# Heads started earlier by swapped buffers, a re-ordered prologue, chunk-wise waits and a final scaling on one engine, in a two-layer encoder trunk

## The chip, the cores and the metric

The kernel runs on one core of one Trainium2 chip. The core has TensorE (PE, matrix products, with its weight loads PEld), VectorE (DVE), ScalarE (ACT), GpSimd (POOL) and SyncE (SP), which here only issues DMAs. The metric is the device time of one execution in microseconds; the figure of a kernel is the median of several runs.

## The reference

Two request groups (prompt and sample), each one sequence of 512 tokens with 1024 features, go through the same two layers and a last RMSNorm. Both groups share all weights.

```python
def trunk(x, c, g_norm, w_ada, b_ada, g_final, even_p, odd_p):
    for l in range(DEPTH):
        mod = jax.nn.silu(c) @ w_ada[l] + b_ada[l]
        shift, scale, gate = jnp.split(mod, 3, axis=-1)
        h = rmsnorm(x, g_norm[l]) * (1 + scale[:, None, :]) + shift[:, None, :]
        j = l // 2
        if l % 2 == 0:
            out = even_mixer(h, *[p[j] for p in even_p])
        else:
            out = odd_mixer(h, *[p[j] for p in odd_p])
        x = x + gate[:, None, :] * out
    return rmsnorm(x, g_final)
...
def odd_mixer(h, w_in1, conv_w, conv_b, w_q, w_k, w_v, w_gate, b_gate, g_mh, skip, w_out1):
    xm, z = jnp.split(h @ w_in1, 2, axis=-1)
    xc = jax.nn.silu(centred_conv(xm, conv_w, conv_b))
    q = headwise(xc, w_q)
    k = headwise(xc, w_k)
    v = headwise(xm, w_v)
    pre = (jnp.concatenate([q, k, v], axis=-1) @ w_gate + b_gate).astype(jnp.float32)
    ...
    h_fwd = mlstm_scan(qh, kh, vh, i_f, jax.nn.log_sigmoid(f_f))
    h_bwd = flip(mlstm_scan(flip(qh), flip(kh), flip(vh), flip(i_b), flip(jax.nn.log_sigmoid(f_b))))
    hs = h_fwd + h_bwd
    ...
    out = (hn.astype(xm.dtype) + skip * xc) * jax.nn.silu(z)
    return out @ w_out1
```

`even_mixer` is one input projection, latent attention with 8 heads, neighbourhood attention with 8 heads, a SiLU gate and an output projection. `odd_mixer` is an mLSTM with 4 heads of 512 features, forward and backward in time, whose head outputs are normalised (`hn`).

## The kernel before

**Tiling.** Every activation is kept with features on the 128 partitions and the 512 tokens of a group in the free dimension (T = 512); x is 8 such chunks (DC = 8), the inner width of the mLSTM 16 (IC = 16). A product of two fp32 operands is made of three products: each operand is split into a high part (ACT, a copy with rounding) and a low part (DVE, a subtraction), and `three` (L483 to L485) multiplies high by high, low by high and high by low. So "hi_..." functions run on ACT, "lo_..." functions on DVE, and PE needs both.

**Weights** come as 81 blocks a group of 128x1024 through a ring of 3 slots (`stream_weights`, L478, SP). `act_split` (L457) writes w_hi and `dve_split` (L465) w_lo, one block each, two in advance (PAIRS = 2). PE multiplies a block with 24 products.

**Order.** There is no scheduler: each engine has a list written out by hand, and semaphores (`wait_ge`, `then_inc`) are all that joins the lists. An instruction that waits holds back everything behind it on its engine. The lists run group 0 (layer 0 in the a_ functions, layer 1 in the e_ functions), then group 1.

**Prologue** (`p_sync`, `p_tensor`, `p_scalar`, `p_vector`). PE transposes vectors (L369, L370), then makes the first modulation in 8 steps k (`ada_step`, L295: 8 product instructions of 2 columns by 512), each when a part of w_ada of 1 MB has come. Between them stand 16 "folds" (`fold`, L361 to L365), which multiply the headwise q, k, v weights into the gate weights; DVE feeds them by `expand` (L410) and stores them by `keep` (L415 to L417). `FOLDS[k]` says how many folds are done after step k. The first mean square is summed over chunks by POOL (`n_gpsimd`, L557, L560) from ACT's squares (`n_square`, L550), and PE adds over partitions by a product with ones (`n_tensor`, L565 and L567) at k = 5. `ada_turn` (L303) and `ada_evict` (L311) end the modulation, `dve_h` and `act_h` (L510, L521, L515) make the first h, and the first projection (L483) starts.

**mLSTM part** (functions inside the e_ part). For each head h PE does: keys (L1461) and token values (L1478) one head in advance, `scores` (kk by xc), `turn` (L1511, transposes of the weighted scores Pn), `values` (pt by v), `back` (L1529). ACT makes `decay` (L1613, L1617; exponentials into the tile Dm, from rows that POOL's `masked` L1389 writes), hi_keys (L1595), hi_values (L1600), pts (L1671), hi_u (L1630). DVE makes `weights(h, i)` (L1776 to L1792; scores times decay, the norm, and the normalised Pn), `stats` (L1798, L1801), lo_keys (L1759), lo_values (L1765), pts low (L1844), scaled_u (L1815), lo_u (L1807). POOL makes `split_x` (L1378, L1380), `skipped` (L1414), `times_z` (L1408) and `norm_factors` (L1396 to L1400). The z half of the input projection runs ahead of the heads and beside head 0: after z block c + 2's products ACT stores SiLU(c) (L1645) and splits the next block. `F_...` constants put gate work between them. Dm lies in the memory of ring slots 1 and 2; so the first decays wait for the last block of the ring (w_lo of block B_OUT1).

**Tail and end.** The last projection (B_OUT1 on, L483 with u_h) needs split blocks and u. `fin_tensor` (L579, L581), `fin_scalar` (L585, L587, L589), `fin_scale` (L597) and `fin_out` (L606) are the last RMSNorm: chunks 0 to 4 are scaled on DVE, 5 to 7 on POOL. For group 0 this runs inside group 1's first blocks.

## Time and profile before

| | |
|---|---|
| time, median of 3 runs | 1626.69 us (1623.75 to 1637.08) |
| time of the profiled execution | 1624.33 us |
| its span, first to last instruction | 1622.5 us |
| mean granted TensorE clock | 0.991 |
| PE busy | 1542.9 us (95%) |
| DVE, ACT, POOL busy | 873.3, 688.7, 375.8 us |
| chain that ended last, by engine | PE 82%, DVE 9%, ACT 5% |
| first projection product starts | 57.91 us |
| last projection product starts | 1606.34 us |

The page gives sums over the whole span. Where time is lost is seen in the waits of PE, a list that says for each line of PE what it waited for, how long in all, how often and how long at most, and in timelines of short stretches. A mean duration in a row with "x8" is the time of all 8.

### The profile page before, as it was taken

To read this page: it belongs to the slowest core of one execution; us is meant where nothing else is said; L and a number is where in the kernel's file an instruction comes from. 1 tells how busy PE (TensorE), PEld (TensorE's weight loads), DVE (VectorE), ACT (ScalarE), POOL (GpSimd) and SP (SyncE) were. 2 spreads that over 40 slices of the span, in tenths; PEclk is the share of its full clock that TensorE was granted. 3 is DMA by queue.
4 is the path that set the end of the run, shared out by engine and by line. 5 is a ranking of instruction groups with operands and counts; after the bars stand their busy time and mean duration, and the time that the engine had idled before them with its cause. 6 is when DMAs were issued, how large, how long until landed. Compare 5 with 4: busy or idle time off the path is not lost.

```text
span 1622.5 us, 19287 instructions
## 1 busy us (share of the span) xinstructions
PE 1542.9 (95%) x7334; PEld 1149.4 (71%) x7334; DVE 873.3 (54%) x1525; ACT 688.7 (42%) x1152; POOL 375.8 (23%) x434
## 2 busy tenths in 40 slices
PE   6999999999999998999999999999999999899996
PEld 4677755668777776777787885566877778677785
DVE  4523236664787427775543324576488751777433
ACT  1323235663533425443544333665443342544333
POOL 2011113332010013564311001342210002265312
PEclk9999999999999999999999999999999999999998
DMA  9288841112322331215334443021342233111421
GB/s 362 90 249 237 280 162 43 43 60 91 130 91 79 120 126 40 49 30 195 93 103 149 130 152 108 30 62 40 100 146 79 92 118 109 45 41 47 148 92 65
DMA packets 68987, 179.51 MB, mean 111 GB/s; under 512 B 20624, under 2 KB 21008, under 8 KB 66848
## 3 DMA queue, kind: packets, MB, share of 16 engines
q1 hardware_dynamic: 68896, 178.29, 34.1%
q8 instruction: 58, 0.95, 0.3%
q14 instruction: 33, 0.27, 0.1%
HBM read 153.59 MB, written 24.67 MB: 110 GB/s over the span
## 4 chain that ended last, share of the span: by engine, by line
PE 82%; DVE 9%; ACT 5%; issue 2%; DMA 1%; SPq 0%; DVEq 0%; ACTq 0%
PE ps L483 20%; PE ps L485 20%; PE ps L484 20%; PE ps L980 3%; PE ps L1029 3%; PE ps L1012 3%; PE ps L997 2%; PE ps L295 2%; DVE w_lo L465 1%; PE ps L911 1%; PE ps L1478 1%; PE ps L1461 1%; ACT w_hi L457 1%; PE ps L1300 1%; DMA at<-w_ada 1%
## 5 line engine op out<-in xcount | busy, mean ns | idle before, releaser
L465 DVE TENSOR_TENSOR w_lo<-at,w_hi 128x1024 fp32r<-128x1024 f32 x162 | 202.6, 1251 | 388.9 <-ACT w_hi L457 388.9
L457 ACT ACTIVATE w_hi<-at 128x1024 fp32r<-128x1024 f32 x162 | 170.4, 1053 | 120.3 <-PE ps L485 120.3
L483 PE MATMUL ps<-h_e_hi,w_hi 128*128 128x512 f32 x480 | 190.9, 398 | 7.9 <-DVE w_lo L465 7.9
L485 PE MATMUL ps<-h_e_hi,w_lo 128*128 128x512 f32 x480 | 187.0, 390 | 0.0
L484 PE MATMUL ps<-h_e_lo,w_hi 128*128 128x512 f32 x480 | 186.9, 389 | 0.0
L483 PE MATMUL ps<-h_a_hi,w_hi 128*128 128x512 f32 x400 | 160.4, 401 | 1.7 <-DVE h_a_lo L515 1.1
L484 PE MATMUL ps<-h_a_lo,w_hi 128*128 128x512 f32 x400 | 157.0, 393 | 0.0
L485 PE MATMUL ps<-h_a_hi,w_lo 128*128 128x512 f32 x400 | 156.8, 392 | 0.0
L1135 POOL TENSOR_SCALAR at<-at,at 128x512 f32<-128x512 f32 x128 | 87.0, 692 | 153.5 <-DVE at L1072 153.5
L483 PEld LDWEIGHTS ps<-h_e_hi,w_hi 128*128 128x128 f32 x480 | 90.1, 188 | 43.8 <-DVE at L1288 11.7
L485 PEld LDWEIGHTS ps<-h_e_hi,w_lo 128*128 128x128 f32 x480 | 90.1, 188 | 19.2
L483 PE MATMUL ps<-u_h_hi,w_hi 128*128 128x512 f32 x256 | 100.4, 392 | 3.4 <-issue 3.4
L484 PEld LDWEIGHTS ps<-h_e_lo,w_hi 128*128 128x128 f32 x480 | 90.2, 188 | 18.2 <-issue 0.5
L485 PE MATMUL ps<-u_h_hi,w_lo 128*128 128x512 f32 x256 | 99.7, 389 | 0.0
L484 PE MATMUL ps<-u_h_lo,w_hi 128*128 128x512 f32 x256 | 99.6, 389 | 0.0
L1288 DVE SCALAR_TENSOR_TENSOR at<-ps,at,at 128x510 f32<-128x510 f32 (+1 forms) x128 | 96.0, 750 | 4.5
L483 PEld LDWEIGHTS ps<-h_a_hi,w_hi 128*128 128x128 f32 x400 | 75.8, 190 | 28.9 <-issue 9.4
L1389 POOL TENSOR_TENSOR at<-at,at 128x512 f32<-128x512 f32 x16 | 22.0, 1395 | 290.8 <-DMA at<-a_rows 290.8
L485 PEld LDWEIGHTS ps<-h_a_hi,w_lo 128*128 128x128 f32 x400 | 75.8, 189 | 16.3
L484 PEld LDWEIGHTS ps<-h_a_lo,w_hi 128*128 128x128 f32 x400 | 75.8, 190 | 15.7 <-issue 0.7
L1012 PEld LDWEIGHTS ps<-at,at 128*128 128x128 f32 x512 | 56.7, 141 | 36.2 <-issue 32.0
L1012 PE MATMUL ps<-at,at 128*128 128x128 f32 x512 | 71.8, 278 | 7.4 <-ACT at L1112 7.2
(257 smaller groups left out, 3024.3 us busy)
## 6 DMA issues: line engine op xcount, KB each, us to landing
at<-blocks_in SPq DMA_DIRECT2D x162, 512.0 KB, 3.7
at<-w_ada SPq DMA_DIRECT2D x32, 512.0 KB, 4.9
at<-w_ada SPq DMA_DIRECT2D x8, 1024.0 KB, 18.5
z_kept<-at SPq DMA_DIRECT2D x32, 256.0 KB, 2.2
at<-z_kept SPq DMA_DIRECT2D x32, 256.0 KB, 2.8
at<-t_masked SPq DMA_DIRECT2D x16, 448.0 KB, 3.3
at<-xs SPq DMA_DIRECT2D x2, 2048.0 KB, 9.6
sg_kept<-at SPq DMA_DIRECT2D x16, 256.0 KB, 4.5
```

What stands on the lines that cost most here:

```text
L295: last = pe.matmul(ps(ADA_BANK[p])[32 * q:32 * q + G], siluc[:, G * k:G * k + G], parts[q], start=(k == 0), stop=(k == DC - 1))
L457: act.activation(whi[:, n % PAIRS], wring[:, n % SLOTS], ACT.Copy).then_inc(sem("w_hi"), 1)
L465: dve.tensor_tensor(wlo[:, n % PAIRS], wring[:, n % SLOTS], whi[:, n % PAIRS].bitcast(F32), ALU.subtract)\
L483: pe.matmul(o, stationary[0], moving[0], start=first, stop=False)
L484: pe.matmul(o, stationary[0], moving[1], start=False, stop=False)
L485: return pe.matmul(o, stationary[1], moving[0], start=False, stop=final)
L980: last = pe.matmul(ps(s_bank(j) + e), qcat[0:QK, u, m * P:(m + 1) * P], kcat[0:QK, u], start=True, stop=True)
L997: last = pe.matmul(ps(s_bank(j + e) + m), naq[a][r:r + 64, n, col:col + P], nak[b][r:r + 64, n], start=(s == 0), stop=(s == 2))
L1012: last = pe.transpose(ps(4 + q)[:, col:col + P], Pt[:, j % 4, e, s * P:(s + 1) * P], ident)
L1029: last = pe.matmul(ps(6 + n % 2)[64 * e:64 * e + 64, 2 * P * half:2 * P * half + 2 * P], v[:, s, (2 * n + e) % HEADS], PT[(j - 1 + e) % 4] ...
L1135: last = pool.tensor_scalar(Pt[:, j % 4, e], Pt[:, j % 4, e], rinv[:, n:n + 1], 1.0, ALU.mult, ALU.mult)
L1288: dve.scalar_tensor_tensor(y[:, lo:hi], src[:, lo + d:hi + d], vb("convw", t * IC + c), y[:, lo:hi], ALU.mult, ALU.add).then_inc(sem("e_co ...
```

## The change

It has six parts.

1. Prologue: `FOLDS` puts more folds ahead and none behind the last modulation; `expand` runs six ahead of `keep`, and the first two `dve_split` stand ahead of keep(14). The mean square is made of eight products with ones on PE, two at each of k = 1 to 4, without POOL. `busy` adds three 128x512 products on a tile of zeros, one ahead of the vector transposes and two behind.
2. The memory of Dm and Pn is swapped. Decays (0,0) and (0,1) move from behind z block 14 to behind z block 13, without the wait for w_lo; decays (1,0) and (1,1) move behind pts(0). On ACT hi_keys(1) goes ahead of decay (0,3), and the split of block B_Z + 17 behind it; its DVE half goes behind weights (0,3). The loads of the last projection wait for the last turn.
3. Token values of head 0 are made in the order 0, 1, 3, 2; `scores` and `values` wait for each chunk of kk and pt instead of for all four.
4. On DVE lo_keys(h+2) and lo_values(h+1) stand ahead of weights(h+1, 3) for h = 0 and 1.
5. Tail: on ACT the split of the second block stands behind the first two hi_u, and the squares of the next x behind the splits.
6. The final scaling is all on DVE, the outputs go out in the order 0 to 7; the 128x1 activations that loaded a table become table loads.

```diff
-    Pn = chunks(take(4 * T, at=L1 + 16 * T), T)
+    Dm = chunks(take(4 * T, at=L1 + 16 * T), T)
...
-    Dm = chunks(take(4 * T, at=ring_lo + 2 * T), T)
+    Pn = chunks(take(4 * T, at=ring_lo + 2 * T), T)
...
-    FOLDS = (1, 4, 6, 8, 10, 12, 14, 14)
+    FOLDS = (4, 6, 8, 10, 12, 14, 16, 16)
...
+        def busy(n):
+
+            for _ in range(n):
+                pe.matmul(ps(4), Weff[:, 0:4], Weff[:, 0:16], start=True, stop=True)
+
+        pe.wait_ge(sem("p_zero"), 2)
+        busy(1)
         pe.wait_ge(sem("p_rows"), 32)
         pe.transpose(ps(0)[:, 0:P], rows[:, 0], ident)
         pe.transpose(ps(0)[:, P:2 * P], rows[:, 1], ident).then_inc(sem("p_vecT"), 1)
+        busy(2)
         pe.wait_ge(sem("p_silu"), 1)
         folded = 0
         for k in range(DC):
             pe.wait_ge(sem(f"p_w{k}"), 16)
             ada_step(pe, 0, k, [ada_w[k][:, q * T:(q + 1) * T] for q in range(4)])
-            if k == 5:
-                groups[0].n_tensor(pe, 6)
+            if 1 <= k <= DC // 2:
+                for c in range(2 * k - 2, 2 * k):
+                    pe.wait_ge(sem("nx_sq"), c + 1)
+                    pe.matmul(ps(6), cst("ones"), nsq[:, c % 2], start=(c == 0), stop=(c == DC - 1))\
+                        .then_inc(sem("nx_add" if c < DC - 1 else "nx_ms"), 1)
             for c in range(folded, FOLDS[k]):
                 fold(c)
             folded = FOLDS[k]
         ada_turn(pe, 0)
-        for c in range(folded, IC):
-            fold(c)
...
+        for c in range(6):
+            expand(c)
         for c in range(IC):
-            expand(c)
-        for c in range(12):
+            if c == IC - 2:
+                for b in range(PAIRS):
+                    groups[0].dve_split(dve, b)
             keep(c)
-        for b in range(PAIRS):
-            groups[0].dve_split(dve, b)
+            if c + 6 < IC:
+                expand(c + 6)
         ada_evict(dve, 0)
-        for c in range(12, 14):
-            keep(c)
         ada_add(dve, 0)
         dve.wait_ge(sem("mod_set"), 3)
         dve.wait_ge(sem("rstd_done"), 1)
         groups[0].dve_h(dve, 0, 0, h_A, xT)
-        for c in range(IC - 2, IC):
-            keep(c)
...
             sp.wait_ge(sem("g_s"), at("g_s", 4 * ML_H))
-            sp.wait_ge(sem("g_P"), at("g_P", 8 * ML_H))
-            sp.wait_ge(sem("g_Pn"), at("g_Pn", 4 * ML_H))
+            sp.wait_ge(sem("g_t"), at("g_t", 4 * ML_H))
             stream_weights(sp, B_OUT1)
...
             def scores(h, part):
-                pe.wait_ge(sem("g_kk"), at("g_kk", 4 * h + 4))
                 pe.wait_ge(sem("g_xs"), at("g_xs", 4 * h + 4))
                 for i in part:
                     if h > 0:
                         pe.wait_ge(sem("g_P"), at("g_P", 8 * (h - 1) + 2 * (i + 1)))
                     for c in range(HC):
+                        if i == 0:
+                            pe.wait_ge(sem("g_kk"), at("g_kk", 4 * h + c + 1))
...
             def values(h):
                 pe.wait_ge(sem("g_v"), at("g_v", 4 * h + 4))
-                pe.wait_ge(sem("g_pt"), at("g_pt", 4 * h + 4))
                 for m in range(TM):
                     for s in range(TM):
+                        if m == 0:
+                            pe.wait_ge(sem("g_pt"), at("g_pt", 4 * h + s + 1))
...
-                if c == IC - 2:
-                    act.wait_ge(sem("w_lo"), at("w_lo", B_OUT1 + 1))
+                if c == IC - 3:
                     decay(0, 0)
                     decay(0, 1)
+            hi_values(0)
             decay(0, 2)
-            hi_values(0)
+            hi_keys(1)
             decay(0, 3)
-            hi_keys(1)
+            act_split(act, B_Z + IC - 1 + PAIRS)
             for h in range(ML_H):
-                if h + 1 < ML_H:
+                if 0 < h < ML_H - 1:
                     decay(h + 1, 0)
                     decay(h + 1, 1)
                 for s in range(TM):
                     act.wait_ge(sem("g_t"), at("g_t", 4 * h + s + 1))
                     act.activation(pts[0][:, s], ps(4 + s), ACT.Copy).then_inc(sem("g_ph"), 1)
+                if h == 0:
+                    decay(1, 0)
+                    decay(1, 1)
...
             act_split(act, B_TAIL + PAIRS)
-            hi_u(ML_H - 1)
+            hi_u(ML_H - 1, (0, 1))
             for b in range(B_TAIL + 1, B_END):
...
                 act_split(act, b + PAIRS)
+                if n == 1:
+                    hi_u(ML_H - 1, (2, 3))
...
                 stats(h, 3)
+                if h + 2 < ML_H:
+                    lo_keys(h + 2)
+                    lo_values(h + 1)
                 if h + 1 < ML_H:
                     weights(h + 1, 3)
                 if h > 0:
                     lo_u(h - 1, (3,))
-                if h + 2 < ML_H:
-                    lo_keys(h + 2)
+                if h + 2 == ML_H:
+                    lo_values(h + 1)
                 if h + 1 < ML_H:
-                    lo_values(h + 1)
                     scaled_u(h)
...
-            for j in range(5):
+            for j in range(DC):
                 LAST.fin_scale(dve, j)
```

Three places of the engines' lists show what stands where. In all of them a line number of the changed kernel differs by a few from the one before; at_... names are memory tiles.

The first is PE's list in the prologue, from its start. Before, L369 and L370 are the vector transposes, L295 a modulation step, L361 to L365 a fold:

```order
L369 MATMUL ps<-at_1808_49,at_256_78 128x128
L370 MATMUL ps<-at_1808_49,at_256_78 128x128
L295 MATMUL ps<-at_2048_70,at_16_54 2x512 x4
L361 MATMUL ps<-at_6144_69 128x128
L362 MATMUL ps<-at_1808_49,at_6144_69 128x128
L363 MATMUL ps<-at_962_79,at_6144_69 128x16
L364 MATMUL ps<-at_962_79,at_6144_69 128x16
L365 MATMUL ps<-at_962_79,at_6144_69 128x16
L295 MATMUL ps<-at_2048_71,at_16_54 2x512 x4
```

The same place of the change (L366 is `busy`, L294 the modulation, L356 to L360 a fold):

```order
L366 MATMUL ps<-at_1024_60 128x512
L371 MATMUL ps<-at_1808_49,at_256_77 128x128
L372 MATMUL ps<-at_1808_49,at_256_77 128x128
L366 MATMUL ps<-at_1024_60 128x512 x2
L294 MATMUL ps<-at_2048_69,at_16_54 2x512 x4
L356 MATMUL ps<-at_6144_68 128x128
L357 MATMUL ps<-at_1808_49,at_6144_68 128x128
L358 MATMUL ps<-at_962_78,at_6144_68 128x16
L359 MATMUL ps<-at_962_78,at_6144_68 128x16
L360 MATMUL ps<-at_962_78,at_6144_68 128x16
```

Behind the fourth fold the second modulation step follows, and behind it the first pair of mean-square products (L382):

```order
L359 MATMUL ps<-at_962_78,at_6144_68 128x16
L360 MATMUL ps<-at_962_78,at_6144_68 128x16
L294 MATMUL ps<-at_2048_70,at_16_54 2x512 x4
L382 MATMUL ps<-at_1024_111,at_1808_49 128x512 x2
L356 MATMUL ps<-at_6144_68 128x128
L357 MATMUL ps<-at_1808_49,at_6144_68 128x128
```

So the mean square's products move from behind step 5 to behind steps 1 to 4, and products on zeros stand ahead of all.

The second is DVE's list at the boundary of heads 0 and 1, from the end of the statistics to scaled_u. Before:

```order
L1798 BN_STATS at_24_158<-ps 128x6
L1801 BN_AGGR at_8_159<-at_24_158 128x2
L1776 SCALAR_TENSOR_TENSOR at_2048_145,at_8_157<-ps,at_2048_145 128x512
L1776 SCALAR_TENSOR_TENSOR at_2048_145,at_8_157<-ps,at_2048_145 128x128
L1782 SCALAR_TENSOR_TENSOR at_8_161<-at_8_157,at_64_156 128x2
L1783 TENSOR_TENSOR at_8_157<-at_8_157,at_8_161 128x2
L1784 RECIPROCAL at_8_157<-at_8_157 128x2
L1788 TENSOR_SCALAR at_2048_140<-at_2048_145,at_8_157 128x512
L1792 SCALAR_TENSOR_TENSOR at_2048_140<-at_2048_145,at_8_157,at_2048_140 128x128
L1759 TENSOR_TENSOR kk_g_lo<-ps,kk_g_hi 128x512 x4
L1765 TENSOR_TENSOR v_g_lo<-ps,v_g_hi 128x512 x4
L1815 SCALAR_TENSOR_TENSOR at_8192_127<-ps,at_128_51,at_8192_127 128x512 x4
```

And now:

```order
L1801 BN_STATS at_24_157<-ps 128x6
L1804 BN_AGGR at_8_158<-at_24_157 128x2
L1762 TENSOR_TENSOR kk_g_lo<-ps,kk_g_hi 128x512 x4
L1768 TENSOR_TENSOR v_g_lo<-ps,v_g_hi 128x512 x4
L1779 SCALAR_TENSOR_TENSOR at_2048_139,at_8_156<-ps,at_2048_139 128x512
L1779 SCALAR_TENSOR_TENSOR at_2048_139,at_8_156<-ps,at_2048_139 128x128
L1785 SCALAR_TENSOR_TENSOR at_8_160<-at_8_156,at_64_155 128x2
L1786 TENSOR_TENSOR at_8_156<-at_8_156,at_8_160 128x2
L1787 RECIPROCAL at_8_156<-at_8_156 128x2
L1791 TENSOR_SCALAR at_2048_144<-at_2048_139,at_8_156 128x512
L1795 SCALAR_TENSOR_TENSOR at_2048_144<-at_2048_139,at_8_156,at_2048_144 128x128
L1818 SCALAR_TENSOR_TENSOR at_8192_126<-ps,at_128_51,at_8192_126 128x512 x4
```

The low halves of keys and values have moved ahead of weights (1,3).

The third is ACT's list around the last z blocks. Before (L1645 is the SiLU, L457 a split, L1613 and L1617 decays, L1600 high values, L1595 high keys):

```order
L1645 ACTIVATE at_1024_144<-ps 128x512
L457 ACTIVATE w_hi<-at_3072_67 128x1024
L1645 ACTIVATE at_1024_144<-ps 128x512
L457 ACTIVATE w_hi<-at_3072_67 128x1024
L1613 ACT_TABLE_LOAD
L1613 ACTIVATE at_2048_145<-at_512_146,at_64_156 128x128
L1613 ACTIVATE at_2048_145<-at_512_147,at_64_156 128x128
L1617 ACTIVATE at_2048_145<-at_1024_148,at_64_156 128x384
L1613 ACTIVATE at_2048_145<-at_512_146,at_64_156 128x128
L1617 ACTIVATE at_2048_145<-at_1024_148,at_64_156 128x128
L1613 ACTIVATE at_2048_145<-at_512_147,at_64_156 128x128
L1617 ACTIVATE at_2048_145<-at_1024_148,at_64_156 128x256
```

Now:

```order
L1642 ACT_TABLE_LOAD
L1642 ACTIVATE at_1024_143<-ps 128x512
L460 ACTIVATE w_hi<-at_3072_66 128x1024
L1642 ACTIVATE at_1024_143<-ps 128x512
L1597 ACTIVATE v_g_hi<-ps 128x512 x4
L1610 ACT_TABLE_LOAD
L1610 ACTIVATE at_2048_139<-at_512_145,at_64_155 128x128
L1614 ACTIVATE at_2048_139<-at_1024_147,at_64_155 128x256
L1610 ACTIVATE at_2048_139<-at_512_146,at_64_155 128x128
L1614 ACTIVATE at_2048_139<-at_1024_147,at_64_155 128x128
L1592 ACTIVATE kk_g_hi<-ps 128x512 x4
L1610 ACTIVATE at_2048_139<-at_512_145,at_64_155 128x128
```

The last SiLU has no decays and no table load ahead of it any more, the high values come directly behind it, the high keys ahead of decay (0,3), and the last split, which stood behind the last SiLU, is not among these rows.

## Rows read from the trace of the kernel before

**Rows 1.** the page's part 1, busy time of each engine

```profile
PE 1542.9 (95%) x7334; PEld 1149.4 (71%) x7334; DVE 873.3 (54%) x1525; ACT 688.7 (42%) x1152; POOL 375.8 (23%) x434
```

**Rows 2.** waits of PE: engine, tile, line <- waited for: us, times, longest

```profile
PE ps L1478 <- DVE kk_g_lo L1759: 9.7, 4, 2.7
...
PE ps L295 <- DMA at<-w_ada: 8.2, 2, 4.4
...
PE ps L1461 <- DVE v_g_lo L1765: 1.9, 1, 1.9
PE ps L483 <- DVE pt_g_lo L1844: 3.7, 2, 1.8
PE ps L483 <- issue: 1.3, 1, 1.3
PE ps L1478 <- ACT at L1645: 3.3, 2, 1.7
PE ps L1511 <- DVE at L1792: 3.2, 2, 1.9
```

**Rows 3.** timeline, PE, prologue: start, us, what [idle before <- releaser]

```profile
8.63 1.89 PE L295 MATMUL ps<-at,at 128*2 128x512 f32 x8 [3.85 <-DMA at<-w_ada]
...
16.95 1.89 PE L295 MATMUL ps<-at,at 128*2 128x512 f32 x8 [4.39 <-DMA at<-w_ada]
...
52.28 1.04 PE L295 MATMUL ps<-at,at 128*2 128x512 f32 x8
...
57.91 0.77 PE L483 MATMUL ps<-h_a_hi,w_hi 128*128 128x512 f32 x1 [1.05 <-DVE h_a_lo L515]
```

**Rows 4.** chain that ended last, prologue: start us, us, what

```profile
24.70 1.81 PE ps L295 x8
30.47 1.81 PE ps L295 x8
...
43.83 2.00 PE ps L565 x2
45.83 1.54 PE ps L567 x2
```

**Rows 5.** windows: stretch, us, busy of PE, PEld, DVE, ACT, POOL, PEclk, DMA

```profile
650.00:700.00 50.00, 45.05 (x211) 35.29 (x210) 35.93 (x86) 21.75 (x42) 33.28 (x44) 0.96 0.19 42
```

**Rows 6.** timeline, ACT, around z block 14's SiLU, group 0

```profile
611.50 0.60 ACT L1645 ACTIVATE at<-ps 128x512 f32<-128x512 f32 x1 [15.12 <-PE ps L485]
...
615.00 0.70 ACT L1613 ACTIVATE at<-at,at 128x128 f32<-128x128 f32 x2 [0.66 <-DVE w_lo L465]
```

**Rows 7.** timeline, PE: scores of head 1, turn of head 1

```profile
629.41 0.50 PE L483 MATMUL ps<-kk_g_hi,xc_g_hi 128*128 128x512 f32 x1 [1.41 <-DVE kk_g_lo L1759]
...
673.51 1.91 PE L1511 MATMUL ps<-at,at 128*128 128x128 f32 x16
```

**Rows 8.** timeline, DVE: weights (1,3), low keys; 128x2 operation elsewhere

```profile
655.02 0.69 DVE L1776 SCALAR_TENSOR_TENSOR at<-ps,at 128x512 f32<-128x512 f32 x1 [1.89 <-PE ps L485]
...
655.97 1.13 DVE L1782 SCALAR_TENSOR_TENSOR at<-at,at 128x2 f32<-128x2 f32 x1
...
659.80 2.47 DVE L1759 TENSOR_TENSOR kk_g_lo<-ps,kk_g_hi 128x512 fp32r<-128x512 f32 x4
...
730.38 0.41 DVE L1782 SCALAR_TENSOR_TENSOR at<-at,at 128x2 f32<-128x2 f32 x1
```

**Rows 9.** timeline, POOL: masks of head 0, xc_g_lo, masks of head 2

```profile
585.89 3.26 POOL L1389 TENSOR_TENSOR at<-at,at 128x512 f32<-128x512 f32 x2 [127.50 <-DMA at<-a_rows]
...
655.82 1.26 POOL L1380 TENSOR_TENSOR xc_g_lo<-at,xc_g_hi 128x512 fp32r<-128x512 f32 x1
...
662.95 2.50 POOL L1389 TENSOR_TENSOR at<-at,at 128x512 f32<-128x512 f32 x2
```

**Rows 10.** DVE: the final scaling's timeline row; durations of L1807 (min/median/max)

```profile
1613.01 6.30 DVE L597 TENSOR_TENSOR at<-at,at 128x512 f32<-128x512 f32 x5 [5.48 <-ACT at L589]
...
L1807 DVE TENSOR_TENSOR u_h_lo<-at,u_h_hi x32: 657/681/1772, 684.5 to 1536.2; 128x512 fp32r<-128x512 f32 x32
```

103 lines of the change are left out of this document (47 added, 56 removed).

## The prediction

> **What bounds the kernel now.** I read the busy times first, then what PE waits for, then single stretches. PE is busy for 1542.9 of 1622.5 us [rows 1], so at most some 80 us can come from waits, and more only where a product itself takes too long. Next, PE's waits [rows 2]: the largest stand in the mLSTM part of each group and in the prologue. They belong to single rows of a list: token values (L1478) wait 9.7 us in 4 places for the low halves of the keys on DVE, 3.3 us for ACT's SiLU; keys (L1461) 3.8 us for the low halves of the values; turn (L1511) 3.2 us for DVE's weights (L1792), values (L483) 3.7 us for pt_g_lo, the last projection 3.4 us ("issue"), the modulation (L295) 8.2 us for w_ada. The counts of 2 and 4 say once or twice per group. Third, the durations in the prologue [rows 3]: the same 8 modulation products take 1.89 us at 16.95 and 1.04 us at 52.28. In the chain [rows 4] they start every 5.77 us (24.70, 30.47): 1.81 for them and 3.96 for two folds, so 1.98 each. The work runs at about half the later pace, 1.2 instead of 2.4 GHz as I read it, until the mean square's two products (43.83 and 45.83, 3.54 us [rows 4]) have ended; from then on everything takes half.
>
> **The change, part by part, for PE's time.**
>
> *Prologue.* Before, PE does modulation k, then folds, and one pair of mean-square products at k = 5; the first projection starts at 57.91 [rows 3]. After, four pairs stand at k = 1 to 4, two folds of 1.98 stand no longer behind the last modulation but ahead of it, and three products on zeros are added at the start. The three zeros' products cost about 1.75 us each at low clock (half of 3.54 [rows 4]); they end before w_ada's first part is there, at 8.63 [rows 3], which hides them; without that cover they would cost 5.3. w_ada's second part lands at 16.95 as before, since loads and their order on SP are the same. From there I go step by step. A k with a pair costs 1.81 + 3.54 + 3.96 = 9.3 at low clock and about half, 4.7, at high; one with two folds alone 5.8 or 3.0; k = 7 has 1.0. After the last modulation come 4.6 us of turn, addition and the first h, as the trace has between 53.3 (52.28 and 1.04) and 57.9 [rows 3]. If the clock is high once the first pair is done: 16.95 + 1.8 + 3.5 + 2.0 = 24.3, three k of 4.7 = 38.4, then 3.0 + 3.0 + 1.0 = 45.4, + 4.6 = 50.0, that is −7.9. If only the second pair raises it: 26.2 after k = 1, 33.5 after k = 2, 42.9, 49.9, + 4.6 = 54.5, −3.4; and +1.4 in either case if k = 0's four folds run at low clock (8.63 + 1.9 + 7.9 = 18.4, past 16.95). If it is high from 16.95 on: 47.4, −10.5. If it never rises: 18.4 + 4 × 9.3 + 2 × 5.8 + 1.8 + 4.6 = 73.5, +15.6. In the trace one pair sufficed, but 20 us of unbroken work stood ahead of it, where the new first pair has a wait. So I take **−5**, the middle of −7.9 and −1.9. The six further products cost 10.5 us at low clock, and that is the part's danger; POOL's sums, which they replace, ran beside PE and give nothing back.
>
> *Start of the heads.* Before, ACT waits for w_lo at 615.00 and does 2.5 us of decays between z block 14 and the last SiLU, for which token values (0) wait 1.7 at the longer place, then keys (1) 1.9 for the values' low halves, and scores (1) start at 629.41 after 1.41 more [rows 2, 6, 7]. After, these decays run behind z block 13, in the 15.12 us in which ACT is idle, and POOL has their masked rows ready (585.89 and 3.26 [rows 9]). Token values and keys run unbroken, −3.6; hi_keys(1) now stands behind decay (0,2) with its table load (about 1.3 + 1.3), ends its first chunk near 625.3, and scores (1), which now wait chunk by chunk, start at 625.5: −3.9. Behind them turn's wait of 1.2 shrinks by 0.7: **−4.6**. Split 66 moves behind decay (0,3); its block is consumed only at the tail. With the swap, Pn lies where blocks stream in later, so on SP the loads for the last projection now wait for the last turn (g_t) instead of the last weights, some 2 us (one turn) later; queued behind them are the last z_back and the next x, and all of them are wanted only after values (3): 0, and 2 if the tail had no slack.
>
> *Boundaries of heads 0 to 1 and 1 to 2.* Before, DVE does weights (1,3) from 655.02 to 659.8, then lo_keys for which token values wait [rows 8]; that wait is 2.4 in the mean, 2.7 at most [rows 2]. After, the low keys follow ACT's chunks at once and PE goes on as soon as the keys' banks are free: the wait goes, and so does part of the low clock behind it (the mean granted clock of this stretch is 0.96 [rows 5], 4 us at half pace, 2 lost). Wait and half pace are 4.4 together; followed through the lists, scores (2) start 3.1 to 3.7 sooner, since the keys' last bank then sets the start. New: weights (h+1,3), 4.8 us, stand behind the low values, which end at about 663.9, so they end at 668.7, and turn, which started at 673.51 [rows 7], wants them at about 669.9. I take **−3.4** per boundary.
>
> *Values of head 3*: the g_pt wait for each chunk removes three of four pt_g_lo operations (3.7 in 2 places [rows 2]): **−1.85**. *Tail*: before, ACT does all of hi_u and two squares ahead of split 68, and PE waits 3.4 in 2 places, 2.1 in the longer [rows 2]; after, split 68 follows two hi_u: **−2.1** in group 0, **−1.3** in group 1.
>
> Group 0: 4.6 + 2 × 3.4 + 1.85 + 2.1 = 15.35. Group 1, which repeats it: 14.55. Together 29.9; I take 28, half a us off for each of four boundaries, because the margin of 1.2 us at turn is thin.
>
> *Final scaling.* DVE's five take 6.30 us beside POOL's three; a two-input product of that shape takes 0.681 alone [rows 10], so eight take 5.4: with the last output then **−1.2** (bounds 0 and −1.6). In group 1 they hide under projections, DVE having room there; uncovered, three more would cost 2.0. The table loads stand in the same places; the 128x1 activation saves 0.1 to 0.2.
>
> **Sum**: −5 −28 −1.2 −0.2 = −34.4 from the profiled 1624.33 us: 1589.9, so 1590. The median shown is 1626.69, the fastest 1623.75; the profiled execution is between, so no shift is made.
>
> **A rule against the change.** DVE's 128x2 operation took 1.13 us at 655.97 and 0.41 at 730.38 [rows 8], and POOL was at two-input work of 1.27 us beside the former [rows 9]. The Trainium skill, "SBUF — State Buffer", section "Who interferes with whom", says that a DVE instruction with two SBUF inputs and a GpSimd instruction that reads SBUF exclude one another for a whole instruction. That agrees with these two rows.
>
> **Rivals.**
>
> (a) *The prologue stays at low clock.* For: 20 us of folds and modulation never raised it, and PE still waits until 16.95. Against: one pair did. Then +15.6 instead of −5: **1610.5**.
>
> (b) *Weights (h+1,3) come late.* POOL's masks at 662.95 take 2.50 for two [rows 9] and more POOL work follows, now beside the moved weights. Uncontended, weights take some 3.3 (the 1.13 would be 0.41, and its 512-wide scaling, lengthened likewise, is about as long as the 0.69 of the first row); with a POOL instruction of 1.27 ahead of three of them, 7.1. Then they end at 671.0, 1.1 after turn wants them, and low clock again costs 1.7 behind such a wait: 4 × 2.8 = 11.2 less gain: **1601**.
>
> (c) *The order does not matter*, because each wait returns at the next dependence. The waits of 1 to 2 us in a row at 616 to 636 speak for that, the chunk-wise waits against. The prologue and end alone stay: **1618**.
>
> (d) *Slower*: DVE falls behind at each boundary, low values waiting for ACT behind decays with weights and scaled_u queued behind. It loses the 13.6 there and adds a stall per boundary; the sum is 1603.5 plus four stalls. Slower than before it gets from 5.2 us a boundary, by over 1% from 9.3. With 8 us and 4 of half pace behind each (2 lost): **1643**. The longest wait in [rows 2] is 4.4, and it is for a DMA.
>
> **Numbers.** Forecast 0.62, (a) 0.13, (b) 0.17, (c) 0.05, (d) 0.03. About 1% (16.2 us) can be told from no change: 1608 to 1641 counts as the same. Forecast and (b) are faster, (a) is split: its own 1610.5 is inside, but falls under 1608 where the heads give 31: 0.06 faster, 0.07 same; (c) same; (d) slower. Faster 0.85, same 0.12, slower 0.03. The low end: −10.5 in the prologue, −33 (all listed waits of the heads and their low clock), −1.8: **1579**. The high end is (a): **1610**.
>
> **What would show it.** Prologue: the first modulation at 8.6 or later, the time of L295 x8 at k = 2, 3 (1.0 or 1.8) and the first projection near 53. Heads: L1478's waits near 0 in both groups, scores (1) near 4 us sooner after the last z block, L1511's wait small (if 4 us or more, (b)). Tail: no "issue" wait over 0.5. End: from the last L589 to the last L597 5.4 us instead of 7. The forecast is wrong if L295 stays at 1.8 past k = 3, or if turn's wait grows by over 2 us in several places.

## The result, and the profile after

| | before | changed |
|---|---|---|
| time, median | 1626.76 us (4 runs, 1623.75 to 1637.08) | 1580.28 us (4 runs, 1578.71 to 1580.83) |
| span of the profiled execution | 1622.5 us | 1578.2 us |
| PE busy | 1542.9 us (95%) | 1529.7 us (97%) |
| mean granted clock | 0.991 | 0.994 |

The ratio is 0.9723, with a 95% interval from 0.9701 to 0.9745: 2.8% faster, 44.3 us by the two spans and 46.5 by the medians, where 34.4 was forecast. The kernel before was run again beside each set of experiments and came out at medians of 1622.3 to 1625.4 us; the experiments are therefore compared with the changed kernel's 1580.28, and where 1 or 2 us matter, by their traces.

The page's first part answers to [rows 1]:

```profile
PE 1529.7 (97%) x7352; PEld 1138.6 (72%) x7352; DVE 873.2 (55%) x1531; ACT 689.2 (44%) x1148; POOL 352.4 (22%) x421
```

PE has 13.2 us less busy time with 18 product instructions more. A change of order alone cannot do that; these are products that no longer run at half clock. PE's waits, the view of [rows 2] (us in total, times, longest):

```profile
PE ps L486 <- DVE w_lo L468: 8.5, 9, 1.3
PE ps L1006 <- ACT at L1106: 7.2, 18, 0.9
...
PE ps L486 <- DVE h_a_lo L518: 3.0, 1, 3.0
...
PE ps L1526 <- DVE v_g_lo L1768: 2.5, 2, 1.3
...
PE ps L486 <- DVE kk_g_lo L1762: 2.2, 2, 1.1
PE ps L1507 <- DVE at L1795: 1.2, 2, 0.6
PE ps L1526 <- ACT at L1619: 1.1, 2, 0.9
```

Two of the rows shown in [rows 2] are those of group 1 alone. Over the whole span of the kernel before, which is what the prediction's text uses, they are:

```profile
PE ps L1461 <- DVE v_g_lo L1765: 3.8, 2, 1.9
PE ps L483 <- issue: 3.4, 2, 2.1
```

The largest row of before, 9.7 us of token values for the low keys, is gone, and with it the waits for the last SiLU, for v_g_lo at the keys, for pt_g_lo and "issue". What heads the list now, 8.5 us for w_lo and 7.2 for L1106, was there before with 8.6 and 7.2 and is not touched by the change. Two rows have grown: h_a_lo, 3.0 for 1.1, since no fold fills that gap now, and back's wait for L1619, which is new.

The prologue on PE, the view of [rows 3]:

```profile
8.46 1.04 PE L294 MATMUL ps<-at,at 128*2 128x512 f32 x8 [1.10 <-DMA at<-w_ada]
...
15.73 1.33 PE L294 MATMUL ps<-at,at 128*2 128x512 f32 x8 [2.10 <-DMA at<-w_ada]
16.99 3.35 PE L382 MATMUL ps<-at,at 128*128 128x512 f32 x4
...
22.18 1.04 PE L294 MATMUL ps<-at,at 128*2 128x512 f32 x8
...
48.21 0.76 PE L486 MATMUL ps<-h_a_hi,w_hi 128*128 128x512 f32 x1 [2.98 <-DVE h_a_lo L518]
```

The first modulation step takes 1.04 us, not 1.89: PE is at the high clock when it starts. Behind the wait of 2.10 at 15.73 it falls once (a pair takes 3.35), and from 22.18 to the end of the modulation everything is at full pace. The first projection starts at 48.21, and behind its wait of 2.98 it begins at half pace, as before.

In the heads, first the window of [rows 5] (stretch, us, busy of PE, PEld, DVE, ACT, POOL, PEclk, DMA share, GB/s):

```profile
650.00:700.00 50.00, 49.79 (x254) 40.77 (x254) 43.82 (x109) 25.60 (x53) 34.63 (x42) 1.00 0.18 53
```

PE's timeline, the view of [rows 7]: scores of head 1, turn of head 0 and turn of head 1.

```profile
617.09 0.47 PE L486 MATMUL ps<-kk_g_hi,xc_g_hi 128*128 128x512 f32 x1 [1.08 <-DVE kk_g_lo L1762]
...
623.44 1.97 PE L1507 MATMUL ps<-at,at 128*128 128x128 f32 x16 [0.62 <-DVE at L1795]
...
656.17 1.91 PE L1507 MATMUL ps<-at,at 128*128 128x128 f32 x16
```

DVE's timeline at the boundary of heads 0 and 1, the view of [rows 8]:

```profile
646.75 0.69 DVE L1768 TENSOR_TENSOR v_g_lo<-ps,v_g_hi 128x512 fp32r<-128x512 f32 x1 [0.20 <-ACT v_g_hi L1597]
...
650.04 0.68 DVE L1779 SCALAR_TENSOR_TENSOR at<-ps,at 128x512 f32<-128x512 f32 x1
...
650.98 1.13 DVE L1785 SCALAR_TENSOR_TENSOR at<-at,at 128x2 f32<-128x2 f32 x1
...
653.75 0.66 DVE L1795 SCALAR_TENSOR_TENSOR at<-at,at,at 128x128 f32<-128x128 f32 x1
```

The granted clock is 1.00 where it was 0.96, and PE is busy for 49.79 of 50 us where it was 45.05. The low values (L1768) and, ahead of them, the low keys now come before weights (1,3), which run from 650.04 to 654.4; turn starts at 656.17, 1.8 us behind them. The 128x2 operation at 650.98 takes 1.13 us as before: it is late in a place where nobody waits.

The end, the view of [rows 10]:

```profile
1570.27 4.91 DVE L599 TENSOR_TENSOR at<-at,at 128x512 f32<-128x512 f32 x8 [5.39 <-ACT at L593]
```

Eight scalings in 4.91 us where five took 6.30.

Where the 44.3 us of the span went is read by milestones, the start of the same products in both traces:

| stretch | before, us | changed, us | difference | forecast |
|---|---|---|---|---|
| start to first projection | 57.91 | 48.21 | −9.7 | −5 |
| to token values (0), group 0 | 558.83 | 560.47 | +1.6 | 0 |
| token values (0) to turn (0) | 19.78 | 14.76 | −5.0 | −4.6 |
| turn (0) to turn (1) | 36.99 | 32.73 | −4.3 | −3.4 |
| turn (1) to turn (2) | 37.51 | 32.64 | −4.9 | −3.4 |
| turn (2) to turn (3) | 25.56 | 25.84 | +0.3 | 0 |
| turn (3) to back (3) | 20.80 | 20.06 | −0.7 | −1.85 |
| back (3) to token values (0), group 1 | 622.90 | 620.37 | −2.5 | −2.1 |
| the same five stretches of group 1's heads | 141.40 | 125.40 | −16.0 | −13.25 |
| back (3) to the end | 100.82 | 97.72 | −3.1 | −2.7 |

The five stretches of group 1 are −7.4, −2.6, −4.9, +0.3 and −1.4. The forecast column adds up to −36.3; the prediction took 1.9 off that for the boundaries.

The first two rows hold for these two executions and vary from one execution to the next. Seven of the experiments below keep the changed kernel's prologue as it is: in their traces the first projection starts at 48.60 to 49.68 and token values (0) at 608.15 to 610.76, where the changed kernel's trace has 48.21 and 608.68. Behind token values (0) the traces are steadier. From there to the end of the span the kernel before needs 1005.76 us and the changed one 969.52, 36.2 less; six experiments that turn out to cost nothing there (nozero, ms_late, keep_high, decays_late, decay02_first, best) lie between 968.78 and 969.68. This stretch, called "from token values (0) to the end" below, is the finest measure for the parts behind the prologue.

### The profile page after: what moved, and what is told of

Same layout as the page of the kernel before. It is cut to its first block, busy times and chain, and to the rows that moved or that the text cites. A ratio compares the mean times of both kernels' runs of the same rounds, so it can differ in the third digit from the quotient of the medians.

```text
span 1578.2 us, 19306 instructions
## 1 busy us (share of the span) xinstructions
PE 1529.7 (97%) x7352; PEld 1138.6 (72%) x7352; DVE 873.2 (55%) x1531; ACT 689.2 (44%) x1148; POOL 352.4 (22%) x421
## 4 chain that ended last, share of the span: by engine, by line
PE 83%; DVE 7%; ACT 4%; DMA 2%; issue 2%; POOL 1%; SPq 0%; DVEq 0%; ACTq 0%; POOLq 0%
PE ps L486 20%; PE ps L488 20%; PE ps L487 20%; PE ps L974 3%; PE ps L1023 3%; PE ps L1006 3%; PE ps L294 2%; PE ps L991 2%; PE ps L1473 1%; PE ps L1456 1%; PE ps L905 1%; DMA at<-w_ada 1%; PE ps L1507 1%; PE ps L1296 1%; DVE w_lo L468 1%
## 5 line engine op out<-in xcount | busy, mean ns | idle before, releaser
L487 PEld LDWEIGHTS ps<-h_a_lo,w_hi 128*128 128x128 f32 x400 | 75.9, 190 | 15.8 <-issue 0.7
```

The lines of the kernel that those rows point to most:

```text
L487: pe.matmul(o, stationary[0], moving[1], start=False, stop=False)
```

## The experiments

Twelve kernels ran. Nine take one part out of the changed kernel or move it, one puts one part alone into the kernel before, and two try to go further. The changed kernel was not timed again beside them, so a difference of 1 or 2 us of the medians is not certain by itself.

### Prologue: what holds the clock

**Without the products on zeros.**

```diff
         pe.wait_ge(sem("p_zero"), 2)
-        busy(1)
...
-        busy(2)
```

> The changed kernel without the three products on zeros. Theory 1 (the products on zeros raise PE's clock before the first modulation step): the step at 8.5 us takes 1.9 us instead of 1.04 and the four folds behind it 7.9 instead of 4, past 15.7, so the first projection starts 2 to 3 us later than 48.21, and the span is 1 to 3 us longer. Rival (they only fill a wait and do nothing): the same durations as now, first projection at 48.2 within 0.3, no difference in time.

Measured: 1582.74 us (1580.78 to 1583.53), 2.5 more than the changed kernel. PE's timeline:

```profile
9.16 1.89 PE L294 MATMUL ps<-at,at 128*2 128x512 f32 x8 [4.20 <-DMA at<-w_ada]
...
18.77 1.89 PE L294 MATMUL ps<-at,at 128*2 128x512 f32 x8
20.59 2.99 PE L380 MATMUL ps<-at,at 128*128 128x512 f32 x4
...
25.42 1.04 PE L294 MATMUL ps<-at,at 128*2 128x512 f32 x8
...
51.45 0.76 PE L484 MATMUL ps<-h_a_hi,w_hi 128*128 128x512 f32 x1 [2.98 <-DVE h_a_lo L516]
```

The steps of k = 0 and k = 1 take 1.89 us each, the first pair ends at the high clock, and the first projection comes at 51.45, 3.2 later than in the changed kernel's trace (0.7 of it because w_ada's first part came later, 9.16 against 8.46) and 1.8 later than in the latest of the other traces with this prologue. So the products on zeros raise the clock, although their results are nothing, and stand in a place where PE would otherwise wait for w_ada. The rival, that they only fill the wait, falls.

**The mean square as before, everything else new.**

```diff
-            if 1 <= k <= DC // 2:
-                for c in range(2 * k - 2, 2 * k):
...
+            if k == 5:
+                groups[0].n_tensor(pe, 6)
...
         def _(pool):
+            groups[0].n_gpsimd(pool)
```

> The changed kernel with the mean square made as before (POOL sums, one pair of products at k = 5), the products on zeros and the order of the folds kept. Theory 1 (the pairs between the steps hold the clock high; modulation and folds alone do not): after the wait at 15.7 the steps k = 1 to 4 come every 5.8 us, the clock rises only with the pair at k = 5, first projection near 54.8, 6.6 us later than 48.21. Rival (a clock once raised comes back by itself some 3.4 us after a wait): steps come every 3 us from about 20 on, and with six products less the first projection starts near 44 to 45, 3 to 4 us earlier.

Measured: 1586.00 us (1584.99 to 1587.27), 5.7 more. PE's timeline:

```profile
8.79 1.04 PE L294 MATMUL ps<-at,at 128*2 128x512 f32 x8 [0.31 <-DMA at<-w_ada]
...
16.04 1.89 PE L294 MATMUL ps<-at,at 128*2 128x512 f32 x8 [2.09 <-DMA at<-w_ada]
...
21.81 1.88 PE L294 MATMUL ps<-at,at 128*2 128x512 f32 x8
40.92 1.92 PE L565 MATMUL ps<-at,at 128*128 128x512 f32 x2
...
45.54 1.04 PE L294 MATMUL ps<-at,at 128*2 128x512 f32 x8
...
54.99 0.77 PE L483 MATMUL ps<-h_a_hi,w_hi 128*128 128x512 f32 x1 [2.98 <-DVE h_a_lo L515]
```

And the window of the thin work (stretch, us, busy of PE, PEld, DVE, ACT, POOL, PEclk, DMA share, GB/s):

```profile
16.00:40.00 24.00, 23.96 (x112) 16.19 (x112) 10.20 (x42) 4.43 (x6) 7.00 (x6) 0.50 0.93 386
```

The zeros still give a fast first step (1.04 at 8.79). After the wait at 16.04 the clock falls and stays down: the granted clock is 0.50 over these 24 us, with steps every 5.77 us through k = 5 while PE works without a gap, until the pair of 128x512 products at 40.92. The first projection starts at 54.99 against 54.8 expected. This is the clearest of the runs: modulation steps (2 columns) and folds keep PE busy but do not bring the clock back in 24 us; one pair of full-size products does. That the clock comes back by itself after a wait, as the rival has it, is wrong for this kind of work. (The rival's 3.4 us is the length of the half-clock stretch in the changed kernel's own trace, where full-size products stand behind the wait: the granted clock is 0.74 over 14.0 to 20.5 us.) The six products that the change adds cost PE some 1 us each at the high clock and are worth 6.8 us at the first projection, 5.3 against the latest of the traces with this prologue.

**Full-size products in both waits of the prologue** (their results are not used):

```diff
+        def hold(n, a, m):
+
+            for _ in range(n):
+                pe.matmul(ps(4), a, m, start=True, stop=True)
...
             folded = FOLDS[k]
+            if k == 0:
+                hold(2, X[:, 1, 0], X[:, 0, 0:4])
         ada_turn(pe, 0)
+        hold(3, X[:, 1, 0], X[:, 0, 0:4])
```

> The changed kernel with five more products whose results are not used: two behind the folds of k = 0, where PE now waits 2.1 us for w_ada, and three behind the turn, where PE waits 3.0 us for the first h. Theory 1 (each of these waits is followed by a stretch at half clock): the step at 15.7 takes 1.04 instead of 1.33 and its pair 2.0 instead of 3.35, first projection near 46.5 and its products at 0.23 us spacing from the start, together 4 us earlier by the second modulation; loads may take 1 to 2 of it back, so 2 to 4 us less in all. Rival (loads of w_ada and of the blocks bound this part anyway): nothing, or up to 1 us slower by the added products.

Measured: 1577.53 us (1577.26 to 1578.17, 4 runs), 2.75 less than the changed kernel, whose fastest run was 1578.71; the ratio to the kernel before is 0.9717 (0.9700 to 0.9733). PE's timeline:

```profile
16.23 1.04 PE L294 MATMUL ps<-at,at 128*2 128x512 f32 x8 [0.27 <-DMA at<-w_ada]
17.20 1.98 PE L387 MATMUL ps<-at,at 128*128 128x512 f32 x4
...
47.05 0.47 PE L494 MATMUL ps<-h_a_hi,w_hi 128*128 128x512 f32 x1 [0.41 <-DVE h_a_lo L526]
47.36 0.40 PE L495 MATMUL ps<-h_a_lo,w_hi 128*128 128x512 f32 x1
```

The pair at 17.20 takes 1.98 instead of 3.35, and the first projection's products take 0.40 instead of 0.63. It starts at 47.05 and not at 46.5, since w_ada's second part came 0.5 us later than in the changed kernel's trace (16.23), and its products then wait for the first h (0.4 us). The time ranges of the two kernels do not overlap. This is the fastest of the kernels that ran, together with the last one below.

**The new prologue alone on the kernel before.**

```diff
-    FOLDS = (1, 4, 6, 8, 10, 12, 14, 14)
+    FOLDS = (4, 6, 8, 10, 12, 14, 16, 16)
...
+        pe.wait_ge(sem("p_zero"), 2)
+        busy(1)
...
-            if k == 5:
-                groups[0].n_tensor(pe, 6)
+            if 1 <= k <= DC // 2:
```

> The kernel before with the whole prologue of the changed kernel and nothing else. Theory (the parts of the change add up): first projection at 48.2, 1.6 to 1.9 us given back under the modulation loads, so 8.1 us less than before, 1616. Rival (the parts depend on one another, so that a later wait takes it up): less than 4 us.

Measured: 1618.80 us (8 runs, 1615.42 to 1622.47) beside 1625.37 for the kernel before (11 runs), 6.6 less, ratio 0.9967 (0.9952 to 0.9982); its span is 1614.9 against 1622.5, 7.6 less. The ratio gives 5.4 us (2.9 to 7.8), so the expected 8.1 is just outside its interval, while the profiled execution has nearly all of it: token values (0) start at 609.00 where before has 616.74, 7.7 sooner, and from there to the end it needs 1005.90 us, before 1005.76. What the prologue gains is not taken up by a later wait. Here its first pair ran at half clock throughout (3.78 us, as in three of the seven other traces with this prologue) and the first projection started at 50.04.

### The heads: which order holds PE

**DVE's order at the boundaries undone.**

```diff
                 stats(h, 3)
-                if h + 2 < ML_H:
-                    lo_keys(h + 2)
-                    lo_values(h + 1)
                 if h + 1 < ML_H:
                     weights(h + 1, 3)
                 if h > 0:
                     lo_u(h - 1, (3,))
+                if h + 2 < ML_H:
+                    lo_keys(h + 2)
```

> The changed kernel with weights(h+1,3) ahead of lo_keys(h+2) and lo_values(h+1) on DVE again. Theory 1 (this order is what the waits at the head boundaries hung on, with the half clock behind them): L1473 waits 2.1 and 2.7 us for kk_g_lo again, two or three of the four token value groups take 5.5 us instead of 3.7, in all 13 to 17 us more than the changed kernel. Rival (decays moved forward and the memory swap did it): under 5 us more.

Measured: 1595.24 us (1592.40 to 1598.25), 15.0 more. The row of PE's waits, and behind it the row of its timeline at the first boundary:

```profile
PE ps L1473 <- DVE kk_g_lo L1762: 9.7, 4, 2.7
```

```profile
648.89 5.46 PE L1473 MATMUL ps<-at,at 128*128 128x128 f32 x32 [2.12 <-DVE kk_g_lo L1762]
```

The row of waits is, to the tenth, the one of before: 9.7 us in 4 places, longest 2.7. From token values to back there are 5.30 us (648.89 to 654.19) where the changed kernel has 3.57 (645.03 to 648.60): the half clock comes back with the wait (granted clock 0.83 in 647 to 657). All four boundaries have these 1.73 us in this trace, so wait and pace are 9.7 + 6.9 = 16.6 us, and from token values (0) to the end it needs 16.7 more (986.24 against 969.52). The profiled execution is the slowest of four that differ by 5.9 us, the median is 15.0 more; that in the faster ones some boundary kept its pace, as one does in the trace of before, would fit but was not seen. This order alone is worth some 15 us.

**Waiting for all four chunks.**

```diff
             def scores(h, part):
+                pe.wait_ge(sem("g_kk"), at("g_kk", 4 * h + 4))
...
-                        if i == 0:
-                            pe.wait_ge(sem("g_kk"), at("g_kk", 4 * h + c + 1))
...
+                pe.wait_ge(sem("g_pt"), at("g_pt", 4 * h + 4))
```

> The changed kernel with scores waiting for all four chunks of kk and values for all four of pt. Theory of the prediction: values (3) wait 1.8 us again in each group and scores (1) about 2 us longer, so 5 to 8 us more. Rival (what stands behind them, back waiting for normalise on ACT and for the low values, was the next bound, so that the wait mostly moves): 0 to 3 us more, and the wait for L1619 behind values (3), now 0.88 and 0.27, goes.

Measured: 1588.36 us (1586.61 to 1589.45), 8.1 more. Of PE's waits:

```profile
PE ps L486 <- DVE kk_g_lo L1760: 5.6, 2, 2.8
PE ps L486 <- DVE pt_g_lo L1847: 3.6, 2, 1.8
```

The waits are 5.6 and 3.6 us where the changed kernel has 2.2 and none: 7.0 more. Back gives 1.1 of it back (its wait for L1619 is gone, as the rival said) and turn 1.2, so 4.7 net. The rest is pace: from back (2) to back (3) this kernel needs 24.87 us (714.20 to 739.07) where the changed one needs 22.51; the waits in it are 1.8 and 0.88, so 1.4 of the 2.36 is work at half clock behind the wait. As much stands behind the longer wait of scores (1): from token values (0) to keys (2) group 0 takes 35.37 us where the changed kernel takes 32.92, and waits explain 1.1 of the 2.45. Four such stretches in the two groups are 5.6 us, with the waits 10.3, and this trace, which is that of the slowest execution, needs 10.0 more from token values (0) to the end (979.55).

**ACT's list around the last z blocks undone**, with the memory swap kept:

```diff
-                if c == IC - 3:
+                if c == IC - 2:
                     decay(0, 0)
                     decay(0, 1)
-            hi_values(0)
-            decay(0, 2)
-            hi_keys(1)
-            decay(0, 3)
             act_split(act, B_Z + IC - 1 + PAIRS)
+            decay(0, 2)
+            hi_values(0)
+            decay(0, 3)
+            hi_keys(1)
```

> The changed kernel with ACT's list around the last z blocks as before: decays (0,0), (0,1) behind z block 14, the last split, decay (0,2), high values, decay (0,3), high keys; the memory swap is kept. Theory: the waits for the last SiLU (1.7), for v_g_lo (1.9) and for kk_g_lo come back, and in group 1 the half clock behind them: 8 to 12 us more. Rival (the wait for w_lo that the swap removed was the cause): under 3 us more, since that wait stays away.

Measured: 1595.34 us (1594.31 to 1596.08), 15.1 more, above the expected 8 to 12. Two rows of PE's waits, token values (0) and the keys of head 1 in its timeline, and the last SiLU in ACT's:

```profile
PE ps L1456 <- DVE v_g_lo L1768: 6.4, 2, 3.2
PE ps L1507 <- DVE at L1795: 6.0, 2, 3.6
```

```profile
610.76 3.73 PE L1473 MATMUL ps<-at,at 128*128 128x128 f32 x32
617.67 5.40 PE L1456 MATMUL ps<-at,at 128*128 128x512 f32 x8 [3.18 <-DVE v_g_lo L1768]
```

```profile
612.17 0.60 ACT L1642 ACTIVATE at<-ps 128x512 f32<-128x512 f32 x1
```

Keys wait 3.18 us and in group 0 then take 5.40 for the work of 3.76 (in group 1 they keep the pace, 3.77), and turn waits for DVE, 3.6 us at most. One of the expected waits did not come back: that for the last SiLU. SiLU begins 1.4 us after token values (0) and they still run unbroken in 3.73 us. The change has a line that the excerpt of its diff does not show: token values wait for each bank's SiLU by itself (`IC - 2 + n` for `IC - 1 if n == 0 else IC`), and by the order 0, 1, 3, 2 the bank of the last SiLU comes last. All the runs here keep this, and none takes it out. Two runs asked which of ACT's moves it is.

**Only decays (0,0), (0,1) late:**

```diff
-                if c == IC - 3:
+                if c == IC - 2:
                     decay(0, 0)
```

> The changed kernel with only decays (0,0) and (0,1) moved back behind z block 14; the order behind the last SiLU stays new. If the decays' place was the main cause at the start of the heads: the wait for the last SiLU is back (about 1 to 1.7 us in each group) and half of start_back's 15 us with it, 6 to 8 us more. If the order of high values, decay (0,2), high keys and the last split was: under 3 us more.

Measured: 1580.43 us (1580.15 to 1582.20), no difference. Of PE's waits:

```profile
PE ps L1507 <- DVE at L1795: 1.3, 2, 0.7
...
PE ps L1456 <- DVE v_g_lo L1768: 1.2, 2, 0.6
...
PE ps L486 <- DVE kk_g_lo L1762: 0.6, 2, 0.3
```

**Only decay (0,2) ahead of the high values:**

```diff
+            decay(0, 2)
             hi_values(0)
-            decay(0, 2)
             hi_keys(1)
```

> The changed kernel with decay (0,2) and its table load ahead of the high values of head 0 instead of behind them; decays (0,0), (0,1) and the last split stay where the change put them. Theory (what costs is ACT's work between the last SiLU and the high values): 2.6 us stand there in place of the 3.6 of start_back, so keys (1) wait 2 us for v_g_lo, and with the half clock behind that wait and the later weights 8 to 12 us more in both groups together. Rival (the split there, or the high keys behind decay (0,3), was what start_back's 15 us came from): under 4 us more.

Measured: 1579.55 us (1578.61 to 1580.83), no difference, where 8 to 12 us had been expected. Of PE's waits:

```profile
PE ps L1456 <- DVE v_g_lo L1768: 2.0, 2, 1.0
...
PE ps L1507 <- DVE at L1795: 1.2, 2, 0.6
```

Both expectations that named one culprit were wrong. The wait for the last SiLU, which the first of them expected, is absent from both. In each of these two the keys wait, 0.6 or 1.0 us in each group, but the scores behind them wait less by as much: with keys, scores and turn together the waits of group 0 are 1.57 us (0.60, 0.31, 0.66), 1.63 (1.02, none, 0.61), and in the changed kernel 1.70 (none, 1.08, 0.62). A few us of ACT's work may stand at one place or another of this chain; what it delays there it does not delay later. Only when all of it stands ahead (late decays, the split, decay (0,2) and its table load), the wait is 3.18, and then pace is lost, and DVE is late for turn too. Which of the combinations of two items already costs was not tried, nor the split alone. In start_back the waits are 6.4 + 6.0 us in both groups, 12.4 against 3.4 in the changed kernel (2.2 + 1.2), so 9.0 us are waits. The pace of group 0's keys is 1.64, and behind the waits of turn each group loses 1.6 or 1.7 (turn (0) to turn (1) takes 34.37 and 34.39 us for 32.73 and 32.72; granted clock 0.89 in 630 to 645). Together that is 14 us, where the stretch from token values (0) to the end is 13.2 longer (982.74 against 969.52). The rest of the 15.3 between the two spans stands ahead of token values (0), where the lists are the same.

### Tail and end

**The squares and all of hi_u ahead of the second split.**

```diff
-            hi_u(ML_H - 1, (0, 1))
+            hi_u(ML_H - 1)
```

> The changed kernel with all four hi_u and the squares ahead of the second split on ACT in the tail, as before. Theory: PE waits 2.1 us (group 0) and 1.3 us (group 1) for that split again, 3.4 us more. Rival (split 67 and the later u chunks bind next): under 1.5 us more.

Measured: 1581.86 us (1581.31 to 1582.34), 1.6 more, where 3.4 was expected. Of PE's waits:

```profile
PE ps L486 <- issue: 1.9, 2, 1.4
```

The wait is 1.9 in both groups together, not 3.4; why the split is less late than before was not traced. From token values (0) to the end this trace needs 2.8 us more (972.28), so the part's worth lies between 1.6 and 2.8.

**The last group's scaling on DVE and POOL.**

```diff
-            for j in range(DC):
+            for j in range(5):
                 LAST.fin_scale(dve, j)
...
+            for j in range(5, DC):
+                LAST.fin_scale(pool, j)
```

> The changed kernel with the last group's final scaling split again, chunks 0 to 4 on DVE and 5 to 7 on POOL, and the outputs in the old order. Theory (POOL's two-input products and DVE's hinder one another): DVE's five take 6.3 us instead of eight in 4.91, and from the first of them to the end of the span it is 9.5 us instead of 7.9; 1.4 to 1.8 us more in all. Rival (the last output DMA sets the end, whichever engine scales): within 0.5 us.

Measured: 1581.91 us (5 runs, 1580.98 to 1582.64), 1.6 more, as expected; span 1579.3, and 1.6 more from token values (0) to the end (971.10). The timeline, and one of DVE's five in a narrow window:

```profile
1569.79 6.29 DVE L599 TENSOR_TENSOR at<-at,at 128x512 f32<-128x512 f32 x5 [5.39 <-ACT at L593]
1569.83 5.10 POOL L599 TENSOR_TENSOR at<-at,at 128x512 f32<-128x512 f32 x3 [8.85 <-ACT at L593]
...
1570.40 1.75 DVE L599 TENSOR_TENSOR at<-at,at 128x512 f32<-128x512 f32 x1
```

Two engines take longer for eight chunks than one: 6.29 us for 4.91 in the changed kernel. DVE's first and last chunk take 0.69 each, as alone; the three between them, beside POOL's three, come every 1.67 us and take 1.74 or 1.75, and POOL's take 1.70 to 1.77.

### One step further

**keep_high, and the low values of head 3 ahead of the last low u of head 1.**

```diff
-                if h > 0:
-                    lo_u(h - 1, (3,))
                 if h + 2 == ML_H:
                     lo_values(h + 1)
+                if h > 0:
+                    lo_u(h - 1, (3,))
```

> keep_high (unused products in the prologue's two waits), and on DVE at head 2 the low values of head 3 ahead of the last low u of head 1. Theory: back (2), which waits 1.27 and 1.26 us for the low values, waits 0.6 less in each group: 1.2 us under keep_high's 1577.5. Rival (PE then waits for the same time at the turn of head 3): the time of keep_high.

Measured: 1577.73 us (1576.93 to 1580.55), the time of keep_high. Of PE's waits:

```profile
PE ps L1515 <- DVE at L1826: 1.4, 2, 0.7
PE ps L1534 <- DVE v_g_lo L1776: 1.3, 2, 0.7
```

Back's wait is 0.66 a group instead of 1.26, as meant, and turn (3) has a new wait of 0.7 a group for scaled_u (L1826): the rival was right. DVE's whole work up to there binds, in whatever order.

## Why the prediction was right, and where its sizes were not

The direction and the main mechanisms hold. The range holds too (1580.28, range from 1579), but only by 1.3 us at the low end, less than the changed kernel's own spread (its fastest execution, 1578.71, lies outside), so that part is luck: the forecast of 1590 was 10 us too slow. Step by step:

**Prologue, −5 forecast; −9.7 at the first projection, −8.1 after the give-back.** The step that failed is the choice between the cases. The first pair's case gives 50.0 and was averaged with a worse one; the trace has 48.21, and the seven other traces with this prologue have 48.60 to 49.68, all a little better than that case. Two things were missed. The products on zeros were priced only as hidden cost; they raise the clock for step 0 and its four folds, which saved k = 0's danger (8.63 + 1.9 + 7.9) outright. And w_ada's second part came at 15.7, 1.2 us sooner than the 16.95 that was said to be unchanged; in the other runs with the same loads it came at 15.8 to 16.5, so it varies by 0.7 us from run to run, and why it is earlier in all of them than in the one trace of before was not tested. Rival (a), a prologue at low clock throughout, fell: nozero and ms_late show the two halves of what keeps it from happening, and even with either gone a later pair brought the clock back.

**What took some of it back.** From the first projection to token values (0) the changed kernel's trace needs 1.6 us more. All of it is lost before 218 us: the last modulation step of this stretch moved from 217.68 to 209.84, 7.8 sooner and no longer 9.7. The modulation steps between stream w_ada in halves, and one of them now has a wait of 0.20 for it that before has not. That an earlier PE runs into the loads there fits that, but was not tested. The seven other traces with this prologue need 558.74 to 561.18 us for the stretch, before 558.83, so the 1.6 is partly that of this one execution; where it goes stays open.

**Start of the heads, −4.6 each; −5.0 and −7.4.** The waits named were right: those for the last SiLU and for the values' low halves are gone, that of scores (1) is 1.08 for 1.41 and that of turn 0.62 for 1.24 and 1.92. In group 1 the sum left out the half clock behind them: keys took 5.40 us there before and take 3.76 now, 1.64, and turn's wait of 1.92 was larger than the 1.24 of group 0. But the reason given, decays in front of the last SiLU, is not what carries it: decays_late costs nothing by itself. For the values' low halves it is the sum of ACT's work ahead of the values and keys (start_back). The wait for the last SiLU, 3.3 us in both groups, stays away even in start_back, so what is left to remove it is the order 0, 1, 3, 2 with its wait for each bank, perhaps with the 0.66 us for w_lo that the swap saves. The prediction gave that order no term, and no run tests it alone.

**Boundaries, −3.4 each; −4.3, −4.9, −2.6, −4.9.** The mechanism was right and dve_order_back shows it row by row. The mis-sized term is pace: I took scores (2) to be held by the last low keys and let 3.1 to 3.7 of 4.4 us through. The trace lets all of it through. Three of the four token value groups took 5.46 or 5.47 us before and take 3.73 now, 1.74 each; the fourth, in group 1, had run at 3.84 already, and there the gain is 2.6, its wait of 2.1 and little more. The margin at turn, 1.2 forecast, is 1.8: the half us a boundary that was taken off was not needed, and rival (b) fell. The contention it rests on is seen, 1.13 us for the 128x2 operation, but only that one instruction was lengthened so (two more, L1786 and L1795, by 0.3 to 0.5 us), not three by a whole POOL instruction each: weights (1,3) took 4.4 us, not 7.1.

**Values of head 3, −1.85 each; −0.7 and −1.4.** The wait for pt_g_lo is gone, but back then waits for L1619, 0.88 and 0.27 us: back transposes what normalise (L1619, ACT) writes, which was ready in time as long as PE stood at the old wait. The sum took the wait's length for the gain. whole_waits has the converse, pt's wait back with 3.6 and L1619's gone.

**Tail −2.1 and −1.3; end −1.2.** Group 0's −2.5 and the last stretch's −3.1 (forecast 1.3 + 1.2 + 0.2) fit. The scaling is 1.39 shorter by the duration rows (6.30 to 4.91), near the lower bound of −1.6, because eight on DVE start 0.61 us apart while one lasts 0.69: consecutive instructions overlap a little. final_back puts it at 1.1 us by spans and 1.6 by medians.

**Rivals (c) and (d)** fell. Order does matter, by 15 us in dve_order_back and in start_back each; yet (c) describes single items of ACT's list well, which cost nothing when moved alone. No stall as in (d) came: the longest wait of PE in the changed kernel's heads is 1.3 us. The parts taken out one by one cost 6.6 (the prologue, put in alone), 15.0, 8.1, 15.1, 1.6 and 1.6 us by medians, 48.0 in all against a gain of 46.5. That they nearly add up does not make them independent. From token values (0) to the end the five taken out cost 16.7, 10.0, 13.2, 2.8 and 1.6 us, 44.3 in all, more than the 36.2 that the whole change gains there; some of the gain is counted in more than one of them. The memory swap and the order of token values were not taken out at all.

On the rule of the Trainium skill that the prediction quoted ("SBUF — State Buffer", "Who interferes with whom": a two-input DVE instruction and a reading GpSimd instruction exclude one another), final_back agrees: on DVE three chunks beside POOL's three take 1.74 or 1.75 us each, those without POOL 0.69. At the boundary it agrees for one instruction and costs nothing, because the moved weights have 1.8 us of room.
